# Prompt attention over eight head pairs: last norms at the edge of a pair, k and v stored in halves, stream chunks earlier, one exp at the head of each pair

## The reference, cut to what matters

```python
q = _rmsnorm(q.reshape(B, T, N_HEADS, HEAD_DIM), q_norm_g)
k = _rmsnorm(k.reshape(B, T, N_HEADS, HEAD_DIM), k_norm_g)
k_all = jnp.concatenate([k_hist, k], axis=1)      # past of the stream, none for the prompt
v_all = jnp.concatenate([v_hist, v], axis=1)
c_all = jnp.cumsum(log forget gates of past and new frames)
s = q @ k_all.T * HEAD_DIM ** -0.5 + c_q - c_k    # per head, masked to k_pos <= q_pos
attn = softmax(s) @ v_all                         # outputs also: the new k (normed) and v
```

## Time and profile before

| | |
|---|---|
| median of 3 runs | 2759.14 us (2758.89 to 2765.78) |
| the profiled execution's own time | 2751.23 us |
| its span, first to last instruction | 2749.7 us |
| mean granted clock of PE | 0.916 |
| attention, first score to the last division (about 185 to 1142 us) | 957 us |

### The profile page before, as it was taken

The page is one execution under the profiler, slowest core; times in us unless marked ns, Lnnn a source line. Parts: engine busy times, 40 slices in busy tenths (PEclk is TensorE's granted clock), DMA queues, the critical chain, the costliest instruction groups (busy, mean ns, idle before and its releaser), DMA issues. The chain is left out here.

```text
span 2749.7 us, 36614 instructions
## 1 busy us (share of the span) xinstructions
PE 2257.4 (82%) x11080; PEld 1748.6 (64%) x11080; DVE 1328.1 (48%) x1548; ACT 1116.7 (41%) x1520; POOL 223.6 (8%) x294
## 2 busy tenths in 40 slices
PE   4459797887979797699899959989917999999991
PEld 2447565665757574499887849975415766666660
DVE  4334444445354444421155542111136888777884
ACT  3223343433333343221155632101105777777770
POOL 0210201202020200000012100000020000000002
PEclk9779898988989897899999979999958999999995
DMA  2210202112020202221156542133036999999986
GB/s 84 64 40 1 79 0 79 29 50 56 24 79 0 63 0 56 77 66 38 51 155 186 185 133 68 46 118 125 0 130 250 387 374 369 366 362 366 377 317 236
DMA packets 207115, 377.28 MB, mean 137 GB/s; under 512 B 20508, under 2 KB 128200, under 8 KB 206968
## 3 DMA queue, kind: packets, MB, share of 16 engines
q1 hardware_dynamic: 184680, 302.07, 32.2%
q0 software_dynamic: 18784, 61.92, 7.1%
q10 hardware_dynamic: 3584, 12.58, 1.2%
HBM read 301.87 MB, written 74.66 MB: 137 GB/s over the span
## 5 line engine op out<-in xcount | busy, mean ns | idle before, releaser
L2132 DVE TENSOR_TENSOR e_w_lo<-e_raw,e_w_hi 128x2048 fp32r<-128x2048 f32 x192 | 438.3, 2290 | 116.1 <-ACT e_w_hi L2059 107.2
L2059 ACT CAST e_w_hi<-e_raw 128x2048 fp32r<-128x2048 f32 x192 | 366.6, 1911 | 142.9 <-DMA e_raw<-w_down_e 60.0
L101 PE MATMUL proj_ps<-w_qkv_hi,xh 128*128 128x384 f32 x544 | 233.0, 428 | 21.6 <-PEq L286 19.2
L1145 PE MATMUL out_ps<-mT 128*128 128x512 f32 (+3 forms) x384 | 181.0, 556 | 23.2 <-ACT mT L1344 18.3
L103 PE MATMUL proj_ps<-w_qkv_hi,xl 128*128 128x384 f32 x544 | 187.9, 345 | 0.0
L102 PE MATMUL proj_ps<-w_qkv_lo,xh 128*128 128x384 f32 x544 | 187.3, 344 | 0.0
L1485 DVE TENSOR_REDUCE neg_part<-max_ps 128x1 f32<-128x512 f32 (+3 forms) x128 | 75.4, 589 | 133.0 <-PE max_ps L1071 72.7
L1344 ACT ACTIVATE mT<-st_ps 128x512 f32<-128x512 f32 x192 | 93.3, 489 | 109.1 <-PE st_ps L1130 48.3
L1671 PE MATMUL m_prod<-m_w_o,mT 128*128 128x512 f32 (+1 forms) x288 | 127.5, 602 | 11.2 <-DMA m_w_o<-w_o 11.2
L101 PEld LDWEIGHTS proj_ps<-w_qkv_hi,xh 128*128 128x128 f32 x544 | 107.2, 197 | 46.2 <-issue 40.7
L101 PE MATMUL e_gate_ps<-e_w_hi,e_xT_hi 128*96 128x512 f32 x256 | 105.8, 413 | 21.2 <-issue 10.5
(11 more groups left out here) (402 smaller groups left out, 5330.3 us busy)
## 6 DMA issues: line engine op xcount, KB each, us to landing
e_raw<-w_gate_e SPq DMA_DIRECT2D x64, 1024.0 KB, 13.8
e_raw<-w_up_e SPq DMA_DIRECT2D x64, 1024.0 KB, 14.1
e_raw<-w_down_e SPq DMA_DIRECT2D x64, 1024.0 KB, 13.0
slot_x<-zrows POOLq DMA_DIRECT2D x48, 440.0 KB, 6.4
e_x<-slot_x SPq DMA_DIRECT2D x33, 384.0 KB, 11.3
w_raw<-w_in SPq DMA_DIRECT2D x24, 512.0 KB, 4.5
slot_y<-e_y ACTq DMA_DIRECT2D x32, 384.0 KB, 6.2
slot_y<-zrows POOLq DMA_DIRECT2D x24, 352.0 KB, 9.6
```

The lines of the kernel that those rows point to most:

```text
L101: nc.tensor.matmul(out, a_hi, b_hi, start=start, stop=False)
L1145: te.matmul(out_ps[u % 2][:, q0 - c * BANK:BANK], v_one[:, j, h, :], probsT[s % 2][:, 0:q1 - q0], start=(j == 0), stop=(s == last_step(u)) ...
L2059: sc.copy(w_hi[u][:, :], w.raw[c][:, :]).then_inc(wh_ready, 1)
L2132: v.tensor_tensor(w_lo[u][:, :], w.raw[c][:, :], w_hi[u][:, :], ALU.subtract).then_inc(wl_ready, 1)
```

## The change

1. The table `SLOTS` is new. `norm 3` moves from step 20 of the pair before to step 1 of the pair itself, and `norm 2` from step 19 to the end of step 23, behind `o`. `qk0 3` goes from step 1 to step 2. The stream's chunks move to earlier steps: `ss 0` from 7 to 5, `ss 3` from 16 to 12, `ss 4` from 18 to 14, with their `sp`; `sw 3` and `sw 4` stay at 19 and 20. `root 1` goes from step 18 to 19, `sum` from step 22 to 21.
2. SP stores k and v of tiles 0 to 3 after the second norm and the rest with the stream's tile after the fourth, each half with a semaphore of its own (six transfers for four). The past keys are loaded ahead of the last third of the weights.
3. POOL does the first `rest_w` earlier, the other two next to each other, and loads the stream's past values and forget sums after the copy of head 1's high part.
4. ACT begins each pair with an exp of one column.

```diff
+    LAST_NORM = 3
+    KV_STORES = (2, 4)
...
-             18: ((("max", 0), ("w", 0)), (("sw", 3), ("ss", 4), ("root", 1))),
-             19: ((("max", 1), ("norm", 2)), (("sp", 4), ("w", 1))), 20: ((("max", 2), ("norm", 3)), (("sw", 4),)),
+             18: ((("max", 0), ("w", 0)), ()), 19: ((("max", 1),), (("sw", 3), ("root", 1))),
+             20: ((("max", 2), ("sw", 4)), (("w", 1),)), 21: ((("max", 3),), (("sum", 0), ("w", 2))),
+             22: ((("rows", 0),), (("qk1", 0),)), 23: ((("qk1", 1),), (("o", 0), ("norm", 2)))}
...
-                def store_kv(p):
-                    sp.wait_ge(kv_ready, p * BATCHES + BATCHES)
+                def store_kv(p, half):
+                    sp.wait_ge(kv_ready, p * BATCHES + 2 * half + 2)
...
+                def step(i, ahead, more):
+                    if more:
+                        sp.wait_ge(w_split, i * 3 + 6)
+                        alone(sp, g)
+                        load_w(sp, g, i + 2, 0)
+                        load_w(sp, g, i + 2, 1)
+                    store_kv(i, 1)
+                    if ahead:
+                        store_kv(i + 1, 0)
+                        probs_turned(i)
+                        load_past_k(i + 1)
+                    if more:
+                        sp.wait_ge(w_split, i * 3 + 7)
+                        alone(sp, g)
+                        load_w(sp, g, i + 2, 2)
+                    store_out(i)
...
+                    sc.activation(warm[:, 2:3], g.ident[:, 0:1], ACT.Exp).then_inc(chain_a, 1)
                     exp(0)
...
-                for n in range(BATCHES):
+                for n in range(LAST_NORM):
                     norm(chain, 0, n)
```

More of the change, by code:

```diff
@@ new lines, in attend @@
+    SLOTS = {0: ((), (("qk0", 2), ("max", 4))), 1: ((("max", 5),), (("max", 6), ("norm", 3))),
+             2: ((("max", 7),), (("rows", 1), ("qk0", 3), ("max", 8))), 3: ((("max", 9),), (("qs", 0), ("max", 10))),
+             4: ((("max", 11),), (("past", 0), ("max", 12))), 5: ((("max", 13),), (("ss", 0), ("max", 14))),
+             6: ((("max", 15), ("sp", 0)), (("past", 1), ("rows", 2), ("out", 0))),
+             7: ((("qk1", 2), ("sw", 0)), (("ss", 1), ("mean", 0))), 8: ((("qk1", 3),), (("sp", 1), ("max", 16))),
+             9: ((("max", 17), ("root", 0)), (("sw", 1), ("past", 2))), 10: ((("max", 18),), (("ss", 2),)),
+             11: ((("max", 19), ("sp", 2)), (("past", 3), ("norm", 0))),
+             12: ((("max", 20), ("sw", 2)), (("ss", 3), ("max", 21))),
+             13: ((("max", 22), ("sp", 3)), (("max", 23), ("norm", 1))), 14: ((("rows", 3),), (("ss", 4), ("out", 1))),
+             15: ((("sp", 4),), (("out", 2),)), 16: ((("qk0", 0),), ()), 17: ((("qk0", 1),), (("mean", 1),)),
+             18: ((("max", 0), ("w", 0)), ()), 19: ((("max", 1),), (("sw", 3), ("root", 1))),
+             20: ((("max", 2), ("sw", 4)), (("w", 1),)), 21: ((("max", 3),), (("sum", 0), ("w", 2))),
+             22: ((("rows", 0),), (("qk1", 0),)), 23: ((("qk1", 1),), (("o", 0), ("norm", 2)))}
@@ L808, in attend @@
     FIRST_MAXES = 4
     NO_TURN = ("max", "out", "mean", "root", "norm", "w", "sum")
-    later = lambda item: item[0] in ("mean", "root", "norm", "w") or item == ("rows", 0) or \
+    later = lambda item: item[0] in ("mean", "root", "w") or item == ("rows", 0) or (item[0] == "norm" and item[1] < LAST_NORM) or \
         (item[0] == "max" and item[1] < FIRST_MAXES) or (item[0] in ("qk0", "qk1") and item[1] < BATCHES // 2)
@@ L913, in _ @@
                 load_w(sp, g, 1, 2)
-                store_kv(0)
+                store_kv(0, 0)
                 for done in g.early:
                     sp.sem_clear(done)
-                with sp.Fori(0, PAIRS - 2) as i:
[L918 to L934, removed]
+                def step(i, ahead, more):
[11 more added lines that the diff above has]
+                        sp.wait_ge(w_split, i * 3 + 7)
+                        alone(sp, g)
+                        load_w(sp, g, i + 2, 2)
+                    store_out(i)
+                with sp.Fori(0, PAIRS - 2) as i:
+                    step(i, True, True)
+                step(PAIRS - 2, True, False)
+                step(PAIRS - 1, False, False)
+                for half in range(2):
+                    sp.wait_ge(kv_stored[half], PAIRS * KV_STORES[half] * 16)
                 sp.wait_ge(pair_stored, PAIRS * 16 + 16)
@@ L1550, in fill @@
                         elif what == "norm":
-                            norm(chain, i + 1, n)
+                            norm(chain, i + 1 if n < LAST_NORM else i, n)
                         elif what == "ss":
```

62 lines of the change are left out of this document (27 added, 35 removed).

## The result

| | before | after |
|---|---|---|
| median of 3 runs | 2759.14 us (2758.89 to 2765.78) | 2685.71 us (2678.88 to 2690.92) |
| ratio, with 95% interval | | 0.9715 (0.968 to 0.975) |
| the profiled execution's own time | 2751.23 us | 2690.92 us |
| mean granted clock of PE | 0.916 | 0.932 |
| first score to last turn of `o` | 951.7 us | 882.8 us |

A forecast was written before the change was run, and what follows sets the result against it. PE, busy 82% of the span, bounds the kernel. Edge gains of 10.9 us less 0.9 elsewhere give 70 over seven pairs; with 2.2 and -1 at the ends, 71 off 2751.2; plus 7.9 for the median, 2688 us (2655 to 2738).

The forecast's parts named there:

- The gap of 2.60 us: Pair's end: PE waits for an exp behind `root 1`'s table loads; moving them was to gain all 2.6 us.
- that of 0.96: PE's gap before `sw 3` at a pair's end; its sooner exp was to gain the whole 0.96 us.
- The gap of 2.83 us: Pair's end: `rows 0` waits for DVE's last maximum behind two norms; gain 2.6 us, bounds 0 to 2.8.
- The gap before `o`: PE's 4.54 us wait at a pair's end; `sum` sooner gains 1.5 us, between 0 and 3.0 by POOL's hold.
- The clock: PE's lower clock around a pair's edge: gain 2.4 of 3.6 us at the end, 0.8 of 2.3 at the head.
- The middle of a pair: Outside the edge, delays from the moved norms and sooner chunks were to cost 0.9 us a pair.
- The prologue: Before the first pair, `norm 3` leaves DVE's way: 2.2 us gained.
- The last pair: With no projection to cover chains, it was to lose 1 us, bounds -3 and +5.
- The head exp: At a pair's head, it only moves a table load into ACT's wait for the first scores: no cost.
- The stores by halves: SP's six stores for four use idle queue time and precede the tile's overwriting: no cost.
- the signs: If right: wait before `o` below 3.5 us, no gap over 1 us at named places, clock near 1.00, pairs of 113 us.
- the signs of a miss: If wrong: waits of 2 us before `sp` or `max 9`, `sum` at 5 us or more, pairs over 118 us.

The follow-up runs named there:

- e2: The changed kernel with the stream's chunks and `root 1` back at their places in the kernel before; 2710.95 us, ratio 0.989 to before.
- e1: The changed kernel with `norm 2` and `norm 3` back at the end of the pair before; 2715.30 us, ratio 0.991 to before.
- e4: The changed kernel with POOL's third split of the weights later, behind the copy of head 1's high part; 2651.92 us, ratio 0.969 to before.
- a0: The changed kernel run and profiled again without an edit; 2673.85 us, ratio 0.971 to before.
- e9: e4 with a table of its own for the last pair, chunks there at the kernel before's places; 2652.29 us, ratio 0.967 to before.
- e3: The changed kernel without the exp of one column at each pair's head; 2668.66 us, ratio 0.974 to before.
- e7: The changed kernel with k and v stored whole after the fourth norm, `norm 3` in the first part of step 1; 2724.18 us, ratio 0.990 to before.
- e5: The changed kernel with `sum` back behind the first `qk1` crossing; 2681.99 us, ratio 0.976 to before.

## Why the prediction was right, step by step

*The gap of 2.60 us* (taken whole) and *that of 0.96* went in full, and e2 brings both back in seven edges. (`sw 3` does not stay at its place, as the list of the change has it: it stood in step 18 and stands in 19.) *The gap of 2.83 us* (2.6 taken) went too; e1 brings it back, larger in six edges, with POOL's hold upon the norms. The prediction missed two waits there. With `sw 3` and `ss 4` no longer in between, PE comes to `max 1` before DVE is through with `mean 1` and `max 0`, and waits 1.20 us. And the wait of 1.14 us before `qk0 1`, which the prediction did not name, went with `ss 3`. So these places brought 6.39 - 1.20 + 1.14 = 6.3 us where 6.2 were taken: the two misses cancel, which is luck.

*The gap before `o`* is a term that was mis-sized: 1.5 us were taken, as half of the way between two ends, and 0.76 came at the second edge. Over the seven edges it was 33.0 - 1.2 - 24.2 = 7.6 us (1.2 of the 33.0 belong to the turn of `o` in the last pair) where 7 x 1.5 = 10.5 were taken, and 3.2 of them came from the seventh, which has no splits. The mechanism was there as described, except that the longest hold fell on the scaling of 128x5, which the prediction's five operations with two tensors leave out. Both ends were right: 1.5 us of wait without a hold (seventh edge and e4), almost no gain with it. The choice of half had no row behind it. The norm that took 1.94 us instead of 0.69 spoke for the full hold, and so did the Trainium skill, page "SBUF — State Buffer", section "SBUF: two separate sides": an operation of DVE that needs the shared pair of ports is blocked for the whole of GpSimd's instruction. The trace agrees: the first operation of `sum`, which reads two tensors, ends at 400.70 + 1.00 = 401.70 us and POOL's second split at 399.33 + 2.35 = 401.68. The scaling behind it ends at 404.46 and the third split at 404.44.

*The clock* was mis-sized the other way: 2.4 of 3.6 us were taken for the end of a pair and 0.8 of 2.3 for the head. The end got all 3.6 (1.00 up to the last weighing), the head nothing: 5.18 us at 0.56 are still 2.3 more than at full clock. Over the whole attention it is 28.8 us of PE's busy time, where 7 x 3.2 = 22 were taken. Seven ends make 25 of it; the fourth pair alone gave 7.1, since before the change it had a further stretch at the lower level, which the prediction used only as the price of a loss:

```profile
554.48:681.27 126.79, 106.52 (x519) 0.89 0.16 44
```

```profile
522.13:635.70 113.57, 99.45 (x519) 0.97 0.17 48
```

Of idle time 40.0 us went, where 7 x (7.7 - 0.9) - 1 = 47 were taken. The two errors cancel, which is luck as well.

*The middle of a pair* cost less than the 0.9 taken: PE's waits from `max 5` to the last maximum ahead of `rows 2` were 1.37, 2.18, 0.87, 0.49 and 0.51 us in the second pair before, 5.4 in all, and are 1.51, 0.26, 0.38, 0.80, 1.07 and 0.49 now, 4.5 in all; a wait of 0.37 us at `ss 1` is new. *The prologue* gave 2.25 us for 2.2. *The last pair* lost 3.0 us where 1 was taken, 4.9 in a0, both within the bounds of -3 and +5. Why stays open: two profiles of one kernel differ there by 1.9 us, more than e9 gains over e4 (1.0). *The head exp* at nothing is right (e3). The stores by halves at nothing are right as well, and e7 shows what the cover was worth: the same store in one piece would have cost over half of the gain. The other loads that SP and POOL now issue in another order were not undone in any run; no wait of PE in the attention is ended by a transfer after the change.

Of the signs, the pair of 113 us and the clock came as told; the wait before `o` stayed above 3.5 us, and a gap of over 1 us came up at `max 1`, a place that the signs do not name. Of the signs of a miss, one came: `sum` takes 5.6 us (400.70 to 404.79 + 1.49), and it stands for the one term that fell short, not for the total.

The parts do not add up. Undone alone, the norms cost 33.8 us, the chunks 17.8 and `sum` 12.2, together 63.8 of 67.2 (951.7 - 884.5); but chunks undone shorten the wait before `o` by 12, and norms undone draw the splits onto themselves. So none of these numbers is the share of a part in the gain.

## What to carry to other kernels

A gap of the busiest engine can cost twice where its clock falls behind it: in e1 and e7 about half of the loss is longer busy time (16 of 34 and 18 of 39 us). It need not: in e5 it is 3 of 12 us, and in e4 the busy time rose by some 3 us while 14 us of waits went. When several gaps stand in a row, price each move against the order in which the others are gone already, not against the gap in the old trace. When a change puts GpSimd's subtractions next to small DVE operations, look at who ends when: a move of one call on POOL brought 9 us.

## What the runs showed of the hardware

The hold by POOL's subtraction falls not only on operations that read two tensors: the `TENSOR_SCALAR` of 128x5, which reads one tensor and a column of factors, took 2.33 us instead of 0.23 (seventh edge and e4) and ended 0.02 us after the subtraction. The reduction and the reciprocal ahead of it ran between two splits and say nothing of this.

The rate at which the experts' weights come differed between three executions whose code in that stretch is the same, 356, 363 and 378 GB/s with the transfers always busy, which moves the end of the program by up to 39 us (608 against 569). The prediction took 0.3% for what a measurement can tell; with this a single execution tells no less than some 2%.
